# A two-direction RWKV-7 scan in chunks: the state's transition over a chunk as one matrix, made for all chunks ahead of the scan

## The reference, cut to what matters

```python
def rwkv7_scan(r, w, k, v, kk, a):
    def step(state, inp):
        r_t, w_t, k_t, v_t, kk_t, a_t = inp
        sa = jnp.einsum('bhvk,bhk->bhv', state, -kk_t)
        state = (state * w_t[:, :, None, :] + sa[..., None] * (kk_t * a_t)[:, :, None, :]
                 + v_t[..., None] * k_t[:, :, None, :])
        return state, jnp.einsum('bhvk,bhk->bhv', state, r_t)
```

## Time and profile before

| | |
|---|---|
| median of 3 runs | 2389.5 us (2381.62 to 2393.41) |
| profiled execution, its own time | 2394.83 us |
| its span | 2392.7 us |
| granted TensorE clock over the span | 0.977 |
| PE busy | 2250.3 us, 94% |
| DVE, ACT, POOL busy | 1246.5, 943.4, 735.8 us |
| the scan's 8 pairs (903.33 to 1372.30 us) | 468.97 us |

### The profile page before, as it was taken

How to read it: one execution, slowest core, us unless ns; L and a number is a source line. 1 busy time by engine, 2 the same in 40 slices (tenths; PEclk the granted TensorE clock), 3 DMA queues, 4 the chain that set the end, 5 groups by cost and what they waited for, 6 DMA issues and landing times.

```text
span 2392.7 us, 46390 instructions
## 1 busy us (share of the span) xinstructions
PE 2250.3 (94%) x19640; PEld 1712.6 (72%) x19640; DVE 1246.5 (52%) x2035; ACT 943.4 (39%) x1681; POOL 735.8 (31%) x384
## 2 busy tenths in 40 slices
PE   8999989999979998988888889999998999999998
PEld 6885778888867647777777777777887666754476
DVE  5028254023155666767777534794213999736123
ACT  4238444233234433444444443554323222343133
POOL 2310334444414203111111033444431433430246
PEclk9999999999979998999999999999997999999999
DMA  4312123233212210000000122343231333222232
GB/s 143 111 60 78 62 72 96 88 101 93 88 42 80 88 44 9 10 10 10 10 10 10 39 71 79 117 179 124 82 106 71 106 117 114 89 87 78 71 94 82
DMA packets 49882, 180.64 MB, mean 75 GB/s; under 512 B 5600, under 2 KB 5856, under 8 KB 49440
## 3 DMA queue, kind: packets, MB, share of 16 engines
q1 hardware_dynamic: 46064, 166.82, 21.6%
q10 hardware_dynamic: 3632, 11.08, 1.2%
HBM read 167.33 MB, written 10.55 MB: 74 GB/s over the span
## 4 chain that ended last, share of the span: by engine, by line
PE 72%; issue 12%; DVE 5%; ACT 5%; POOL 4%; DMA 0%; POOLq 0%; ACTq 0%; DVEq 0%; SPq 0%
PE ps L603 15%; PE ps L604 15%; PE ps L605 15%; PE ps L606 6%; POOL ring_lo L2266 4%; PE ps L904 2%; PE ps L865 2%; PE ps L651 2%; PE ps L895 1%; PE ps L1101 1%; PE ps L722 1%; PE ps L737 1%; PE ps L712 1%; PE ps L1122 1%; PE ps L813 1%
## 5 line engine op out<-in xcount | busy, mean ns | idle before, releaser
L2266 POOL TENSOR_TENSOR ring_lo<-ring,ring_hi 128x1024 fp32r<-128x1024 f32 x240 | 589.8, 2465 | 1019.1 <-ACT ring_hi L1158 1019.0
L605 PE MATMUL ps<-u_lo,ring_hi 128*128 128x512 f32 x968 | 384.8, 398 | 0.0
L1158 ACT ACTIVATE ring_hi<-ring 128x1024 fp32r<-128x1024 f32 x240 | 251.4, 1052 | 105.4 <-DMA ring<-in_wall 102.0
L603 PE MATMUL ps<-mlp_u_hi,ring_hi 128*128 128x512 f32 x512 | 204.6, 400 | 13.6 <-DVE u_lo L1744 9.0
L606 PE MATMUL ps<-arena,ring 128*128 128x512 f32 x480 | 210.5, 594 | 6.0 <-ACT arena L1627 3.3
L605 PEld LDWEIGHTS ps<-u_lo,ring_hi 128*128 128x128 f32 x968 | 183.9, 190 | 43.5
L603 PE MATMUL ps<-mid_hi,ring_hi 128*128 128x512 f32 x512 | 203.3, 397 | 2.6 <-POOL ring_lo L2266 2.6
L604 PE MATMUL ps<-mlp_u_hi,ring_lo 128*128 128x512 f32 x512 | 203.2, 397 | 0.0
L605 PE MATMUL ps<-mid_lo,ring_hi 128*128 128x512 f32 x512 | 202.5, 396 | 0.0
L604 PE MATMUL ps<-mid_hi,ring_lo 128*128 128x512 f32 x512 | 202.5, 395 | 0.0
L603 PE MATMUL ps<-in_u_hi,ring_hi 128*128 128x512 f32 x480 | 193.8, 404 | 5.8 <-POOL gs_lo L2354 2.8
(11 more groups left out here) (434 smaller groups left out, 4335.6 us busy)
## 6 DMA issues: line engine op xcount, KB each, us to landing
ring<-in_wall SPq DMA_DIRECT2D x273, 512.0 KB, 3.7
s_tables<-arena ACTq DMA_DIRECT2D x16, 512.0 KB, 2.7
arena<-s_tables SPq DMA_DIRECT2D x16, 512.0 KB, 3.7
arena<-bias_lines SPq DMA_DIRECT2D x16, 448.0 KB, 4.3
arena<-in_lora SPq DMA_DIRECT2D x8, 384.0 KB, 3.0
h<-in_x SPq DMA_DIRECT2D x1, 2048.0 KB, 8.0
out<-arena ACTq DMA_DIRECT2D x8, 256.0 KB, 2.9
consts<-in_consts SPq DMA_DIRECT2D x1, 1152.0 KB, 14.1
```

What stands on the lines that cost most here:

```text
L603: nc.tensor.matmul(y, w_hi, high, start=x == 0, stop=False)
L605: return nc.tensor.matmul(y, w_hi, low, start=False, stop=x == k - 1)
L1158: nc.scalar.activation(ring_hi[:, slot], ring[:, slot], ACT.Copy).then_inc(sem("weights_high"), 1)
L2266: G.tensor_tensor(ring_lo[:, slot], ring[:, slot], ring_hi[:, slot].bitcast(F32), ALU.subtract).then_inc(sem("weights_split"), 1)
```

## The change

The recurrence over a chunk is S' = decay·(S + ka·(v part) + be·u), with u = T·(Ma·v + al·S). The changed kernel splits u into a part without the state, T·Ma·v, and a part that is linear in it, Q = T·al. Both are made for all chunks at once ahead of the scan. From Q it makes step = 1 + Q·be (the state's transition over a chunk) and adds Q·M to ro (so that an output needs one product with the state). A state step is then: the chunk's added part (state_added), one product step·S on top of it, and one copy by ACT with the decay as its scale (Identity). DVE is out of the steps.

Ahead of the scan this needs new work: al turned (each_turned_al, two groups, the first together with the centring of v, which is moved here from level 5); Ma·v within the last level (last_inner); T·[Ma·v, al] with 128 columns (joined); the products of Q with the turned features for six chunks (C, the diff's loop over range(1, NCH - 1)), those with M0 or M1 for seven (A); copies of each by ACT or DVE and two additions by DVE. Moved besides: the variances of the pair before from behind the scores into level 1; the gate product from 8 quarters in the steps to two whole products of 512 columns, one in level 5 and one behind it; the bonus product now as 64x64 products of 128 columns, in the steps 1 to 4; the masks of direction 1 behind level 4's first update. One of three exponentials of a direction's decays and a subtraction are gone, the second direction's decays move into the scan, and the table sets of ACT are loaded by hand: one load for logarithm and exponential together, and the sigmoid's at the end of the scan. The stream of weights behind the scan brings two blocks after the last level and the others only after the last outputs.

```diff
         feats = [[{name: home[6 * d + n] for n, name in enumerate(FEATURES)} for d in range(2)] for home in homes]
-        R = [{name: over_mixes[8 + 4 * d + n] for n, name in enumerate(["Ma", "M0", "M1", "T"])} for d in range(2)]
+        R = [{"T": over_mixes[12 + d], "L": of_ring[4 + d], "X": of_ring[6 + d], "TT": of_ring[d]} for d in range(2)]
+        o_sb, dev = beside[2:4], beside[4:6]
+        joined = [arena[:, pair0 + (8 + 2 * d) * SEQ:pair0 + (10 + 2 * d) * SEQ].rearrange("p (n s) -> p n s", n=2)
+                  for d in range(2)]
...
+            R[d]["Ma"], R[d]["alT"] = over_mixes[8 + 2 * d], over_mixes[9 + 2 * d]
+            R[d]["M0"], R[d]["M1"] = [over_mixes[14:16], beside[0:2]][d]
+            R[d]["Q"], R[d]["step"], R[d]["S"] = R[d]["Ma"], R[d]["alT"], R[d]["T"]
+        v_u = [[sq[:, e * SEQ:(e + 1) * SEQ] for e in range(2)], of_ring[2:4]]
...
-            stream(FIRST_BLOCK["o"], b0 + RING)
+            stream(FIRST_BLOCK["o"], FIRST_BLOCK["o"] + 2)
+            sp.wait_ge(sem("o_ready_rw"), 2 * DT)
+            stream(FIRST_BLOCK["o"] + 2, b0 + RING)
...
+            def each_turned_al(d, F, v=None):
+                for c in range(NCH):
+                    for e in range(2):
+                        rows, crossed, at = slice(e * HEAD, (e + 1) * HEAD), slice((1 - e) * HEAD, (2 - e) * HEAD), slice(c * CH, (c + 1) * CH)
+                        if v is not None:
+                            mm = nc.tensor.matmul(O[0][rows, at], v[rows, at], const("center", 0, CH)[rows, :], start=True, stop=True)
+                            if c == NCH - 1 and e == 1:
+                                mm.then_inc(sem("scores_ready"), 1)
+                        mm = nc.tensor.matmul(A[d][crossed, at], F["al"][rows, at], const("eye", 0, CH)[rows, :], start=True, stop=True)
+                mm.then_inc(sem("scores_ready"), 1)
+            def last_inner(d):
+                for c in range(NCH):
+                    for e in range(2):
+                        rows, crossed, at = slice(e * HEAD, (e + 1) * HEAD), slice((1 - e) * HEAD, (2 - e) * HEAD), slice(c * CH, (c + 1) * CH)
+                        mm = nc.tensor.matmul(A[d][rows, at], R[d]["L"][rows, at], R[d]["T"][rows, at], start=True, stop=True)
+                        if c == NCH - 1 and e == 1:
+                            mm.then_inc(sem("x_ready"), 1)
+                        mm = nc.tensor.matmul(C[d][crossed, at], R[d]["Ma"][rows, at], v_u[0][e][rows, at], start=True, stop=True)
+                mm.then_inc(sem("inner_ready"), 1)
...
                 if prev:
-                    out_variances(prev)
+                    pe.wait_ge(sem("o_copied"), prev(2, 1))
+                each_turned_al(0, F[0], pair_tile(vTr, n))
+                each_turned_al(1, F[1])
...
-                        each(A[d], R[d]["L"], R[d]["T"]).then_inc(sem("x_ready"), 1)
+                        if l < LEVELS - 1:
+                            each(A[d], R[d]["L"], R[d]["T"]).then_inc(sem("x_ready"), 1)
+                        else:
+                            pe.wait_ge(sem("turned"), n(4, 2 * d + 1))
+                            last_inner(d)
+                    if nxt and l == LEVELS - 1:
+                        pe.wait_ge(sem("turned"), n(4, 2))
+                        hidden_product(nxt, 2, 0, 3)
...
+                        if prev and l == 1 and d == 1:
+                            pe.wait_ge(sem("v_turned"), n(1, 1))
+                            out_variances(prev)
...
+                def of_step(j, d):
+                    c = j if d == 0 else NCH - 1 - j
+                    return c, slice(c * CH, (c + 1) * CH)
+                def state_added(j, d, alone):
+                    _, at = of_step(j, d)
+                    for e in range(2):
+                        mm = nc.tensor.matmul(B[d][e * HEAD:(e + 1) * HEAD, at], F[d][("ka", "be")[e]][:, at], v_u[d][e][:, at],
+                                              start=True, stop=alone)
+                    return mm
+                def outputs(j, d):
+                    _, at = of_step(j, d)
+                    for e in range(2):
+                        rows = slice(e * HEAD, (e + 1) * HEAD)
                         if j:
...
+                            nc.tensor.matmul(O[d][rows, at], R[d]["S"][rows, at], F[d]["ro"][rows, at], start=True, stop=False)
+                    for e in range(2):
+                        rows = slice(e * HEAD, (e + 1) * HEAD)
+                        mm = nc.tensor.matmul(O[d][rows, at], v_u[d][e][:, at], R[d][("M0", "M1")[e]][:, at],
+                                              start=j == 0, stop=True)
+                    return mm
+                for d in range(2):
+                    pe.wait_ge(sem("t_updated"), n(10, 2 * (LEVELS - 2) + d + 1))
+                    pe.wait_ge(sem("inner_taken"), n(6, 3 + d))
+                    for j in range(NCH):
+                        c, at = of_step(j, d)
+                        for e in range(2):
+                            crossed = slice((1 - e) * HEAD, (2 - e) * HEAD)
+                            mm = nc.tensor.matmul(ps[crossed, 4 * d * SEQ + c * 2 * CH:4 * d * SEQ + (c + 1) * 2 * CH],
+                                                  R[d]["T"][crossed, at], joined[d][crossed, :, at], start=True, stop=True)
+                    mm.then_inc(sem("inner_ready"), 1)
+                for d in range(2):
+                    if d == 0:
+                        pe.wait_ge(sem("inner_taken"), n(6, 5))
+                    else:
+                        pe.wait_ge(sem("inner_added"), n(6, 1))
+                    pe.wait_ge(sem("turned"), n(4, 2 * d + 2))
+                    for j in range(1, NCH - 1):
+                        _, at = of_step(j, d)
                         for e in range(2):
                             rows, crossed = slice(e * HEAD, (e + 1) * HEAD), slice((1 - e) * HEAD, (2 - e) * HEAD)
...
+                            mm = nc.tensor.matmul(C[d][rows, at], R[d]["Q"][crossed, at], F[d][("ka", "be")[e]][crossed, at],
+                                                  start=True, stop=True)
+                    mm.then_inc(sem("inner_ready"), 1)
+                for d in range(2):
+                    if d == 0:
+                        pe.wait_ge(sem("inner_taken"), n(6, 6))
+                    else:
+                        pe.wait_ge(sem("inner_added"), n(6, 2))
+                        pe.wait_ge(sem("v_copied"), n(2, 2))
+                    state_added(0, d, True).then_inc(sem("s_ready_rw"), 1)
+                    for j in range(1, NCH):
+                        _, at = of_step(j, d)
+                        for e in range(2):
+                            rows, crossed = slice(e * HEAD, (e + 1) * HEAD), slice((1 - e) * HEAD, (2 - e) * HEAD)
+                            mm = nc.tensor.matmul(A[d][rows, at], R[d]["Q"][crossed, at], R[d][("M0", "M1")[e]][crossed, at],
+                                                  start=True, stop=True)
+                    mm.then_inc(sem("inner_ready"), 1)
+                if nxt:
+                    pe.wait_ge(sem("z_taken"), nxt(6, 6))
+                for j in range(1, NCH):
+                    if j == 1:
+                        for d in range(2):
+                            outputs(0, d)
                     for d in range(2):
...
+                        _, at = of_step(j, d)
+                        pe.wait_ge(sem("state_ready"), n(14, 2 * (j - 1) + d + 1))
+                        if j == NCH - 1:
+                            continue
+                        state_added(j, d, False)
+                        if j == 1:
+                            pe.wait_ge(sem("inner_added"), n(6, 3 + d))
                         for e in range(2):
                             rows = slice(e * HEAD, (e + 1) * HEAD)
...
+                            mm = nc.tensor.matmul(B[d][rows, at], R[d]["step"][rows, at], R[d]["S"][rows, at], start=False, stop=True)
+                        mm.then_inc(sem("s_ready_rw"), 1)
                     for d in range(2):
...
+                        if j == 2:
+                            pe.wait_ge(sem("inner_added"), n(6, 5 + d))
+                        if j > 1:
+                            outputs(j - 1, d)
+                    if j < 5:
+                        bonus_quarter((j - 1) // 2, 2 * ((j - 1) % 2))
+                        bonus_quarter((j - 1) // 2, 2 * ((j - 1) % 2) + 1)
+                for d in range(2):
+                    outputs(NCH - 1, d).then_inc(sem("o_ready_rw"), 1)
...
+                for d in range(2):
+                    act.wait_ge(sem("inner_ready"), n(8, 1 + d))
+                    taken(R[d]["Ma"], bank(4 * d + 2), "inner_taken")
+                if nxt:
                     for d in range(2):
...
+                        if prev:
+                            act.wait_ge(sem("dir_gated"), prev(2, d + 1))
+                        feature(nxt, G, 2, d, 3)
+                act.wait_ge(sem("inner_ready"), n(8, 3))
```

(51 more changed lines are left out.)

365 lines of the change are left out of this document (137 added, 228 removed).

## The result

| | before | after |
|---|---|---|
| median, us | 2391.45 (2381.62 to 2393.68, 4 runs) | 2421.86 (2419.32 to 2425.28, 4 runs) |
| profiled execution: time, span, us | 2394.8, 2392.7 | 2425.28, 2423.5 |
| eight pairs in the profile, us | 468.97 | 499.65 |

The ratio is 1.0136 with a 95% interval of 1.0104 to 1.0168: the change makes the kernel 1.4% slower. The forecast was 2427: 38 us more were expected, 30.4 came.

The account below looks back on a forecast made before the run. PE was taken to bound the kernel, filling the scan and level 1. Terms summed to 5.1 us a pair, 41 for eight; less the edges, +38 on the median of 2389.5 gave 2427 us, range 2378 to 2450.

Parts of the forecast that it names:

- The scan: Scan of a middle pair: 8.0 us ahead of the steps plus 15.4 of steps, 23.4 against 22.61, +0.8.
- 0.15 for a change of shape: PE in the scan steps: each change of the products' tile shape costs 0.15 us, eight changes in steps 2 to 4.
- the first rival: Scan steps: a lone pair of products isn't charged for its shape; 2376 us, or 2364 without the supply's share; chance 0.15.
- DVE's small operations: Scan: DVE's small copies and decays go, having cost nothing and gaining nothing, since PE was busy.
- Scores and level 1: Start of a pair: scores -0.6, variances in level 1 +2.0, direction 1's T +0.5, masks of Ma +0.5 us.
- Level 4: Level 4: direction 1's masks stand behind the first update and its transposition, so PE waits, about +0.9 us a pair.
- Level 5: Level 5: two gate products come in (2.2 us), turned v (0.95) and 1.8 of idle time go, -0.6 a pair.
- Supply of instructions: Behind the scores and in level 5: instructions arrive at 128 records in 3.6 us, +1.6 us a pair, bounds 0 and 2.5.
- The pair's 5.1: Sum of all terms for a middle pair, 5.1 us longer; times eight, 41.
- DVE behind POOL: Levels 3 and 4: POOL's feature products hold DVE's transpositions, 20 us more, 2447; chance 0.15.
- The edges: Outside the pairs: a table load behind the last pair goes (1.3 us), and about 1 us ahead of the first.
- The last pair: Last of the eight pairs, with no gate product to move: left at the mean growth, though losing more in the scan.

Follow-up runs that it names:

- e1: Changed kernel with each scan step's products reordered to two changes of shape: scan 18.42 us instead of 23.05, median 2390.1 us, ratio 0.9986 to the kernel before.
- e2: Changed kernel with scan products reordered to four changes of shape in steps 2 to 4: scan 19.59 us, whole 2401.7 us.
- e4: Kernel before with its bonus product in 64x64 tiles, two at a time: scan 22.12 us instead of 22.46, whole 2384.97 us in one execution.
- e10: Changed kernel with 96 records turning v and al replaced by 12 copying records ahead of level 1 (values differ): whole 2418.3 us, 3.5 less.
- e6: Changed kernel with the variances' products cut from 512 columns to 32 (values differ): scores and level 1 10.68 us instead of 12.10, whole 2414.5 us.
- e11: Changed kernel with level 5's 64 records of Ma with v replaced by 8 (values differ): level 5 7.28 us instead of 8.38, whole 2412.4 us.
- e8: Kernel before with its scores issued twice, 128 more records a pair: scores 7.8 us instead of 4.56, whole 2422.9 us.

## Why the prediction came true

**The scan.** Forecast 23.4, measured 23.05. Stretch ahead of the steps 8.0, measured 7.80 (1066.44 to 1074.24, where the first outputs start); step 1 1.8, measured 1.73; a step with bonus 2.6, measured 2.55; one without 1.84, measured 1.86 (1083.61 to 1085.47); the steps together 15.4, measured 15.25. The step of the sum that carried it, 0.15 for a change of shape, holds for groups of four records too: 0.144 to 0.147 by e1 and e2. That rules out the first rival, a lone pair that isn't charged, and shows what the change left lying: DVE is out of the steps, but the scan has 53 changes of shape where the old one has 37, and lasts as long as before. What the Trainium skill says without a price (TensorEngine Tiling (Array Packing), Tiling Modes, Key Properties: a change of the tiling mode drains TensorE) agrees with these runs (0.147 us a change).

**DVE's small operations** I had as costing and gaining nothing, because PE was busy. e4 shows that this was too simple: with ten changes fewer the old scan ran into DVE's copy behind its slowed decays. It didn't alter the sum, since PE bound both scans for the most part; but e4's order made the old scan only 0.3 us shorter (1.6 in two pairs), and e1's made the new one 4.6 shorter. That is what the change really brings, as far as shown: no other order of the old scan was tried.

**Scores and level 1.** Forecast -0.6 + 2.0 + 0.5 + 0.5 = +2.4, measured +2.6. The sum is right, its split isn't. The scores, forecast 0.6 shorter, got 0.2 longer (4.56 to 4.74 by the median), since the supply's gap stands there; level 1, forecast 3.0 longer, got 2.4 longer. Taken at another cut it comes out clean. The hidden product of level 1 starts 7.48 us into a pair before and 8.1 after (median): +0.6, of which 0.4 is DVE's masks (7.88 in e10) and the rest the supply. From there to the end of level 1 it is 2.01 before and 4.02 after: +2.0, the variances (1.92, and e6 shows that they aren't hidden).

**Level 4.** Forecast +0.9 for the masks of direction 1, measured -0.1 (7.26 to 7.13 by the median). This term was wrong. The masks (1.25) end at 1057.7 in pair 2, ahead of the last half product's update at 1058.02, and DVE stands idle for 0.28 there. Over the eight pairs PE waits for these masks 2.3 us, 0.3 a pair, and level 4's idle time with no releaser falls from 1.42 to 0.72 (mean of pairs 1 to 6), which more than covers it.

**Level 5.** Forecast -0.6, measured +1.6. The step that failed is the idle time. I took PE's work to grow by 1.25 (2.2 for the gate product less 0.95 for the turned v) and 1.8 of idle time to go. The mean idle time of level 5 over pairs 1 to 6 was 1.26 before, 0.88 behind ACT's copies and 0.38 with no releaser, and is 1.62 after, all of it with no releaser: 1.25 + 0.36 is the +1.6 measured.

**Supply of instructions.** Forecast +1.6 a pair (0 to 2.5), measured as PE's idle time with no releaser +1.4 (mean of pairs 1 to 6, 2.0 to 3.4; over all eight 16.3 to 27.0 us). The two places that I had named are the right ones: +0.6 in the scores and +0.25 in level 1, +1.2 in level 5, against -0.7 in level 4. What it costs differs: e11 takes 1.1 out of level 5 by cutting 56 records there, while e10, cutting 84 behind the scores, gains 0.2 in place, where DVE's masks come next, and 0.6 in level 5. I read 128 records in 3.6 us off two gaps; e8 measures 3.3 as a cost.

**Luck in the sum.** Levels 4 and 5 and the supply together: forecast 0.9 - 0.6 + 1.6 = +1.9, measured +1.8 over levels 3 to 5. That these agree is in part luck: level 4's term was 1.0 too high and level 5's 2.2 too low, of which at most the supply's 1.6 was entered elsewhere. The pair's 5.1 (measured 4.9 by the medians, 4.7 by the means) rests on this; the scan and the variances came out term by term.

**DVE behind POOL**, the third rival, did not occur. POOL makes features from 1051.53 to 1056.9 in pair 2; the timeline of DVE in the changed kernel has its transpositions in that time at 0.71, as elsewhere:

```profile
1052.23 0.71 DVE L2160 STREAM_TRANSPOSE ring<-arena 128x512 f32<-128x512 f32 x1
...
1055.85 0.71 DVE L2160 STREAM_TRANSPOSE ring<-arena 128x512 f32<-128x512 f32 x1
```

e4's decays (0.41 and 1.45 for two) show that other operations do suffer. The Trainium skill (GPSIMD Engine Reference, Specifications) puts the contention on DVE's two-port mode or two SBUF inputs; the transpositions agree with it. Why two small decays triple is not told apart here.

**The edges.** Behind the last pair one table load is gone. ACT's timeline of the changed kernel has this one, for logarithm and exponential together:

```profile
1406.38 1.28 ACT L1631 ACT_TABLE_LOAD   x1
```

From the last copy of outputs to the copy of y it was 12.2 us (1372.30 to 1384.49) and is 10.0 (1404.24 to 1414.20): -2.2, forecast -1.3. Ahead of the first pair I forecast -1; the pairs begin 1.4 later (904.75 instead of 903.33), but in e10 and e11, which have the same code up to there, they begin at 902.5 and 900.4. That term can't be read from single executions. The last pair, which I left at the mean of 5.1, got 3.3 longer. This and the first pair, 1.1 shorter, are most of why eight times 4.9 came out as 31 and not as 39, and why 30.4 came of the 38 forecast.

## What to carry to other kernels

Count the changes of TensorE's tile shape as well as its products: a step whose products follow in the same order of data, but sorted by shape, took 1.67 us instead of 2.55. Count its instructions too, and look for gaps on TensorE that nothing released: in such a stretch 128 more matmul records cost 3.3 us (e8) and 56 fewer, by products of 512 columns in place of 64, gave 1.1 back (e11). Where the stretch's end waits for another engine, fewer records give next to nothing (e10). And before a scan is rebuilt, look for a copy that stands behind work for which nobody waits yet: moving two logarithms on ScalarE (with one table load less a pair), and one product into the neighbours' shape, brought more (0.6%) than the new scan did in its better order (0.1% in e1).

## What the runs showed of the hardware that I had not expected

- A change of shape of TensorE's tile (128x64 to 64x64 or the other way) costs the same 0.15 us for one pair of products as for a group of four, and the same scan with 53, 29 and 21 changes took 23.05, 19.59 and 18.42 us.
- 128 extra records that write what is there already lengthened a stage by 3.3 us, though PE needs 2.0 for them, and TensorE stood 1.46 us with nothing to wait for that the profile shows. Such pauses lie at or just under a multiple of 128 records behind one another (762, 128, 761, 507, 128, 254, 762 in the changed kernel).
- Level 5 got 1.3 us shorter in one pair while PE's busy time in it grew by 0.5, from 6.54 to 7.01 us, since 56 records fewer had to arrive.
- Two 128x64 decays on DVE took 0.41 us alone and from 0.63 to 1.45 with GpSimd busy, while a 128x512 transposition stayed at 0.71 beside it.
